# The third dense unit of six stages gets weight tiles of its own, split right behind the norm

## The chip, the cores and the metric

The kernel runs on one core of a Trainium2 chip. Five engines work side by side and meet by semaphores: TensorE (PE in the profile, its weight loads PEld) multiplies, VectorE (DVE), ScalarE (ACT) and GpSimd (POOL) do the elementwise work, SyncE (SP) issues most of the DMAs. The metric is the time of one launch on the device in microseconds. The kernel before takes 1724.36 us, the median of three runs (1722.74 to 1725.32).

## The reference

One step of a two-layer trunk, in float32, on 640 tokens (512 of a latent grid, 128 of a context). Width 1024, FFN width 2816. The two token groups share all weights and differ in their modulation. Cut to what matters:

```python
def trunk_layer(x, mod, g_mix_pre, g_mix_post, g_ffn_pre, g_ffn_post, w_ffn_in, w_ffn_conv, w_ffn_out, mixer):
    shift1, scale1, gate1, shift2, scale2, gate2 = mod      # silu(c) @ w_mod + b_mod
    h = rmsnorm(x, g_mix_pre) * (1 + scale1) + shift1
    y, ctx_state = mixer(h)          # h @ w_in, attention (layer 0: also pooling), @ w_out
    x = x + gate1 * rmsnorm(y, g_mix_post)
    h = rmsnorm(x, g_ffn_pre) * (1 + scale2) + shift2
    x = x + gate2 * rmsnorm(conv_ffn(h, w_ffn_in, w_ffn_conv, w_ffn_out), g_ffn_post)
    return x, ctx_state

def conv_ffn(h, w_in, w_conv, w_out):
    u = h @ w_in                     # then 3 taps along the tokens
    gate, val = jnp.split(u, 2, axis=-1)
    return (jax.nn.silu(gate) * val) @ w_out
```

## The kernel before, in words

**Units.** Activations lie feature-major: 8 chunks of 128 features by 640 tokens. A dense stage is cut into *units*, each 128 output features for all tokens; units are numbered through the program (`UNITS`). A stage is, in each layer, the input projection ("in", 12 or 18 units), the mixer's output ("mix", 8), the first half of the FFN's gate and value columns ("fin0", 22), its down projection ("fout0", 8), and the second halves ("fin1", "fout1").

**Three products for one.** Weights and activations are held as a high part (rounded to the multiplier's format) and a low residual; a product is high x high + high x low + low x high. So a unit over 8 chunks is 8 x 3 x 2 = 48 matmuls, the 2 being the two halves of 320 tokens, which go to two PSUM banks (`bankA[s]`, `bankB[s]`). The high part of a weight is a ScalarE copy (`hi`, L519 to L523, into `whi`), the residual a VectorE subtraction (`lo`, L836 to L840, into `wlo`).

**Two slots.** `raw`, `whi`, `wlo` and the bank pairs have two slots, and unit u uses slot s = u mod 2. For unit u, SyncE loads `raw[s]` once `lo` of unit u-2 is done (`s_lo`); `hi` waits until unit u-2 has been multiplied (`s_unit`), `lo` for `hi` (`s_hi`), TensorE for `lo` and for both halves of unit u-2 to be read out of the banks (`s_fa`, counted by ScalarE's `copy_a`; `s_fb`, counted by VectorE's `copy_b`). In a running stage the split of unit u+2 therefore happens while unit u+1 is multiplied. Each engine works off its own program in order, so the code of an engine is its queue: ScalarE's body of a pair is, for each slot, wait for the unit, `hi` of the unit after next, then the bank copy; VectorE's is bank copy, then `lo`, then what the stage adds.

**The start of a stage.** In the input projections and in "fin0" the activations come chunk by chunk out of `pre_norm`, in "mix" out of the split of the mixer's output (`mix_in_hi`, `mix_in_lo`). The first two units are multiplied together, chunk by chunk as these arrive (`first_pair`, `mix_pair`, `pair_chunk` L1619): for a chunk six matmuls of slot 0, then six of slot 1. Both units thus end within six matmuls of each other, and the third unit, which uses slot 0 again, can be split only then.

**What else hangs on it.** Behind `pre_norm` of layer 0, ScalarE runs a SiLU over a wide copy of the conditioning vector (`wide_silu`, L635 to L637); VectorE waits for it (`s_cwsilu`) before its modulation products (`mod_chunk`, L843 to L850), which fill layer 0's stages; in "mix" of layer 0 four of them (two chunks) follow each unit's split. A change of ScalarE's function set is a table load in its program. The loops over pairs are hardware loops (`Fori`).

Of the kernel before, what the change touches and what calls it, by code (L numbers as in the profile page):

```python
# [26 lines left out]
F32 = mybir.dt.float32  # L27
# [36 lines left out]
ADDED = ((0, "mix"), (0, "fout1"), (1, "mix"), (1, "fout1"))  # L64

# [46 lines left out]
UNITS_OF = attention_units()  # L112

# [5 lines left out]
def program(nc, a, o):  # L119
    with ExitStack() as ctx:  # L120
# [88 lines left out]
        assert pos[0] <= region_f + 2 * FH * NT * 4  # L209
        cwide1 = at("cwide1", [P, 2, 1024], F32, region_c)  # L210
# [307 lines left out]
        def _(act):  # L518
# [5 lines left out]

            def pairs(phase, evac):
# [107 lines left out]
            pre_norm(0, 0, True)  # L633

# [8 lines left out]
            def unit_pair(pair, dsts, k2=KD, scale=1.0):  # L643
                for s in range(2):
                    act.wait_ge(s_unit, 2 * pair + (s + 3))
                    hi(s, k2, pair + 1)
# [78 lines left out]
            def mix_in_hi(layer):  # L725

                act.wait_ge(s_oe, (30, 70)[layer])
                for c in range(KD):
                    nc.scalar.activation(hh[:, c, :], y[:, c, :], ACT.Copy).then_inc(s_oth, 1)
                load_sqrt()  # L730
# [59 lines left out]
            pre_norm(0, 2)  # L790
            wide_silu(cwide1, 2)
# [3 lines left out]
            pre_norm(1, 0)  # L795


            p1 = UNITS[(1, "in")][0] // 2
            with act.Fori(0, 4) as h:
# [28 lines left out]
            pre_norm(1, 2)  # L828
            ffn(1)
# [4 lines left out]
        def _(dve):  # L834
            V = nc.vector

            def lo(s, kk, u):

                dve.wait_ge(s_hi, u + 1)
                V.tensor_tensor(wlo[:, s, 0:kk * P], raw[:, s, 0:kk * P], whi[:, s, 0:kk * P].bitcast(F32),  # L840
                                ALU.subtract).then_inc(s_lo, 1)
# [22 lines left out]
            def run(phase, evac, after=None):  # L864
# [6 lines left out]
                def body(h, k2, extra):  # L871
                    for s in range(2):
                        u = 2 * h + (u0 + s)
                        dve.wait_ge(s_unit, u + 3)
                        evac(h, s, u, lambda: lo(s, k2, u + 2) if k2 is not None else None)
                        if extra is not None:
                            extra(h, s)
                if knext == kk and after is None:
                    with dve.Fori(0, n // 2) as h:
                        body(h, kk, None)  # L880
                else:
                    with dve.Fori(0, n // 2 - 1) as h:
# [3 lines left out]
            def run_all(phase, evac, after):  # L886
# [4 lines left out]
                for k in range(n):  # L891
# [4 lines left out]
                    evac(h, s, u0 + k, lambda: lo(s, k2, u0 + k + 2) if k2 is not None else None)  # L896
# [14 lines left out]
            def unit_pair(pair, dsts, k2=KD, after=None, scale=None):  # L911
                for s in range(2):
                    dve.wait_ge(s_unit, 2 * pair + (s + 3))
                    copy_b(dsts[s], s, scale)
                    lo(s, k2, 2 * pair + (s + 2))
# [108 lines left out]
            pre_norm(0, 0, True)  # L1024

# [12 lines left out]
            def first_early():  # L1038
                for s in range(2):
                    dve.wait_ge(s_unit, s + 3)  # L1040
                    copy_b((apad[s][:, PAD + HT:PAD + NS], apad[s][:, AP0:AP0 + NP]), s)
                    lo(s, KD, s + 2)
# [136 lines left out]
            def mix_in_lo(layer):  # L1179
# [5 lines left out]
                for c in range(KD):  # L1185
                    low(c)

# [111 lines left out]
            pre_norm(0, 2)  # L1299
            ffn(0)  # L1300
            post_norm(0, 3)
            pre_norm(1, 0)
            p1 = UNITS[(1, "in")][0] // 2
# [41 lines left out]
            pre_norm(1, 2)  # L1345
            ffn(1)
# [154 lines left out]

# [456 lines left out]
```

## Time and profile before

| | |
|---|---|
| median of three runs | 1724.36 us |
| span of the profiled execution | 1720.7 us |
| what lies around the span, against the median | 3.7 us |
| TensorE busy | 1601.5 us, 93% of the span |
| VectorE busy | 1097.6 us, 64% |
| ScalarE busy | 716.9 us, 42% |
| GpSimd busy | 132.3 us, 8% |
| HBM traffic | 93 GB/s over the span |

The profile is one execution; its times are microseconds from the first instruction. The profiled execution has no time of its own beside its span, so the table sets it against the median. A matmul's row shows its whole way through the array, 0.31 us for 320 columns, while the next one starts about 0.15 us after it; so a busy TensorE in this table is a TensorE that always has a matmul under way. In brackets behind an instruction stands the idle time of its engine just before it and who ended it.

### The profile page before, as it was taken

How to read it: one execution, taken by the hardware profiler on the slowest of the kernel's cores; microseconds unless marked ns; L12 is line 12 of the kernel's file. 1: busy time of each engine (PE TensorE's matmuls, PEld its weight loads, DVE VectorE, ACT ScalarE, POOL GpSimd, SP SyncE). 2: the span in 40 equal slices, each digit the busy share in tenths (PEclk: the TensorE clock that was granted, in tenths of full speed). 3: DMA queues.
4: the chain of work that ended last, by engine and by line, in shares of the span. 5: the costliest groups of instructions: out<-in, count | busy, mean ns of one | idle time of the engine just before them, and what ended most of it. 6: DMA issues, size and time to landing. Idle time of an engine off the chain costs nothing.

```text
span 1720.7 us, 31763 instructions
## 1 busy us (share of the span) xinstructions
PE 1601.5 (93%) x11837; PEld 1535.5 (89%) x11837; DVE 1097.6 (64%) x2060; ACT 716.9 (42%) x1189; POOL 132.3 (8%) x133
## 2 busy tenths in 40 slices
PE   7798998879999999999889979989799999999996
PEld 4797887869999999999879967779699999999996
DVE  5796766957777767778853248853666642466534
ACT  6532664264443134442251147652565531344410
POOL 1431110010000000000100032500100000000001
PEclk9898999999999999999999989999999999999998
DMA  9233002503334533345422120102022221222211
GB/s 362 83 127 106 2 2 92 193 10 117 115 112 165 177 120 110 110 144 188 147 80 73 62 65 2 45 7 80 13 75 81 79 85 61 71 73 74 91 67 61
DMA packets 43773, 160.33 MB, mean 93 GB/s; under 512 B 5184, under 2 KB 6208, under 8 KB 43440
## 3 DMA queue, kind: packets, MB, share of 16 engines
q1 hardware_dynamic: 40896, 152.00, 26.5%
q0 software_dynamic: 1584, 6.38, 1.1%
q8 instruction: 49, 0.80, 0.2%
q10 hardware_dynamic: 1216, 0.92, 0.2%
q14 instruction: 28, 0.23, 0.0%
HBM read 155.74 MB, written 3.54 MB: 93 GB/s over the span
## 4 chain that ended last, share of the span: by engine, by line
PE 76%; DVE 10%; issue 4%; ACT 2%; DMA 2%; POOL 0%; ACTq 0%; DVEq 0%; POOLq 0%; SPq 0%
PE ps L1498 28%; PE ps L1499 28%; PE ps L1676 4%; PE ps L1705 3%; PE ps L1533 3%; PE ps L1691 3%; DMA work<-in_wmodt 2%; DVE work L848 2%; PE ps L1625 1%; PE ps L1626 1%; DVE wlo L840 1%; DVE work L927 1%; DVE ring L848 1%; DVE x L961 1%; PE ps L1512 1%
## 5 line engine op out<-in xcount | busy, mean ns | idle before, releaser
L523 ACT ACTIVATE whi<-raw 128x1024 fp32r<-128x1024 f32 (+1 forms) x166 | 185.7, 1121 | 578.7 <-PE ps L1499 495.9
L1498 PE MATMUL ps<-hh,whi 128*128 128x320 f32 x928 | 288.7, 311 | 15.3 <-DVE wlo L840 15.3
L1499 PE MATMUL ps<-hh,whi 128*128 128x320 f32 x928 | 287.9, 310 | 0.0
L1498 PE MATMUL ps<-hl,whi 128*128 128x320 f32 x928 | 287.7, 310 | 0.0
L1499 PE MATMUL ps<-hl,whi 128*128 128x320 f32 x928 | 287.7, 310 | 0.0
L1499 PE MATMUL ps<-hh,wlo 128*128 128x320 f32 x928 | 287.7, 310 | 0.0
L1498 PE MATMUL ps<-hh,wlo 128*128 128x320 f32 x928 | 287.7, 310 | 0.0
L840 DVE TENSOR_TENSOR wlo<-raw,whi 128x1024 fp32r<-128x1024 f32 (+1 forms) x166 | 218.4, 1318 | 74.8 <-ACT whi L523 74.5
L1498 PEld LDWEIGHTS ps<-hh,whi 128*128 128x128 f32 x928 | 175.1, 189 | 17.1 <-DVE wlo L840 17.1
L1498 PEld LDWEIGHTS ps<-hl,whi 128*128 128x128 f32 x928 | 175.3, 189 | 0.0
L1499 PEld LDWEIGHTS ps<-hh,whi 128*128 128x128 f32 x928 | 175.2, 189 | 0.0
L1498 PEld LDWEIGHTS ps<-hh,wlo 128*128 128x128 f32 x928 | 175.1, 189 | 0.0
L1499 PEld LDWEIGHTS ps<-hh,wlo 128*128 128x128 f32 x928 | 175.0, 189 | 0.0
L1499 PEld LDWEIGHTS ps<-hl,whi 128*128 128x128 f32 x928 | 175.0, 189 | 0.0
L689 ACT ACTIVATE pb<-pb,stat 128x640 f32<-128x640 f32 (+3 forms) x140 | 92.1, 660 | 9.6 <-DVE stat L1120 9.5
L768 ACT ACTIVATE work<-work,wconv 128x642 f32<-128x642 f32 x88 | 73.5, 835 | 52.9 <-DVE work L905 34.7
L1498 PE MATMUL ps<-ffh,whi 128*128 128x320 f32 x308 | 95.2, 309 | 0.0
L1499 PE MATMUL ps<-ffh,whi 128*128 128x320 f32 x308 | 95.2, 309 | 0.0
L1498 PE MATMUL ps<-ffl,whi 128*128 128x320 f32 x308 | 95.2, 309 | 0.0
L1499 PE MATMUL ps<-ffl,whi 128*128 128x320 f32 x308 | 95.2, 309 | 0.0
L1498 PE MATMUL ps<-ffh,wlo 128*128 128x320 f32 x308 | 95.2, 309 | 0.0
L1499 PE MATMUL ps<-ffh,wlo 128*128 128x320 f32 x308 | 95.2, 309 | 0.0
(219 smaller groups left out, 3169.6 us busy)
## 6 DMA issues: line engine op xcount, KB each, us to landing
raw<-in_w SPq DMA_DIRECT2D x134, 512.0 KB, 3.5
work<-in_wmodt SPq DMA_DIRECT2D x54, 512.0 KB, 3.6
raw<-in_w SPq DMA_DIRECT2D x32, 704.0 KB, 4.2
ring<-in_wmodt SPq DMA_DIRECT2D x26, 512.0 KB, 3.7
work<-in_wmod SPq DMA_DIRECT2D x16, 512.0 KB, 6.0
work<-in_rpb POOLq DMA_DIRECT2D x8, 448.0 KB, 4.2
x<-in_x SPq DMA_DIRECT2D x8, 320.0 KB, 6.6
out_x<-x SPq DMA_DIRECT2D x8, 320.0 KB, 2.2
```

What stands on the lines that cost most here:

```text
L523: nc.scalar.activation(whi[:, s, 0:kk * P], raw[:, s, 0:kk * P], ACT.Copy).then_inc(s_hi, 1)
L689: nc.scalar.activation(probs, probs, ACT.Exp, bias=negm, scale=-1.0, accum_out=sums[:, job.unit, half:half + 1]).then_inc(s_p, 1)
L768: nc.scalar.activation(cb[s], ub[s][:, 1:1 + CW], ACT.Copy, scale=wconv[:, bass.ds(2 * h + (2 * f0 + s), 1), 1]).then_inc(s_c1, 1)
L840: V.tensor_tensor(wlo[:, s, 0:kk * P], raw[:, s, 0:kk * P], whi[:, s, 0:kk * P].bitcast(F32), ALU.subtract).then_inc(s_lo, 1)
L848: last = V.scalar_tensor_tensor(out=out, in0=ring[b], scalar=1.0, in1=cwide[:, st, :], op0=ALU.mult, op1=ALU.mult, accum_out=mod[:, st, ba ...
L927: V.tensor_tensor(tn[s], chunk(src, k), inverse_rows, ALU.mult).then_inc(s_t, 1)
L1498: T.matmul(bankA[s], slot(w, s, k), h[:, k, 0:HT], start=st, stop=sp_)
L1499: last = T.matmul(bankB[s], slot(w, s, k), h[:, k, HT:NT], start=st, stop=sp_)
L1533: last = T.matmul(out, h[:, k, t * P:(t + 1) * P], w[:, :, k * P:(k + 1) * P], start=k == 0 and n == 0, stop=k == KD - 1 and n == 2)
L1676: ins = T.matmul(scores_of(job, c, c + w), q[job.rows, job.pair, job.q0:job.q0 + P], k[job.rows, job.kslot, k0:k0 + w], start=n == 0, stop ...
L1691: T.transpose(turned_probs[half][:, c:c + P], pb[j % 4][:, c:c + P], ident[:, :])
L1705: T.matmul(values_bank[job.rows, 0:P], v[:, t, job.v_col:job.v_col + DH], pts[:, job.half, c:c + P], start=i == 0, stop=i == len(keys) - 1)
```

## The change

Two new tiles, `third_hi` and `third_lo`, are laid over a stretch of the FFN region that no one uses at the starts of these stages. In six stages ("in", "mix" and "fin0" of both layers; `THIRD` lists the units) the third unit is split into them: ScalarE runs `hi_third` right behind the norm's last high part or behind the mixer output's, VectorE runs `lo_third` right behind the last residual. The waits on the slot's previous unit (`s_unit`) fall away for it. TensorE multiplies that unit from the new tiles (`third`), still in banks of slot 0, and still behind `s_fa` and `s_fb`. The usual `hi` and `lo` are left out for these six units, and the first round of the loops concerned is written out in front of them on ScalarE, VectorE and TensorE. Amounts of work are the same.

```diff
+THIRD = [UNITS[p][0] + 2 for p in ((0, "in"), (0, "mix"), (0, "fin0"), (1, "in"), (1, "mix"), (1, "fin0"))]
...
+        third_hi = at("third_hi", [P, KD * P], F32R, region_f + 4 * 3840)
+        third_lo = at("third_lo", [P, KD * P], F32R, region_f + 4 * 3840 + 4 * KD * P)
...
+            def hi_third(u):
+
+                act.wait_ge(s_raw[0], 16 * (u // 2) + 16)
+                nc.scalar.activation(third_hi[:, :], raw[:, 0, 0:KD * P], ACT.Copy).then_inc(s_hi, 1)
+
...
-                        if k2 is not None:
+                        if k2 is not None and not (isinstance(h, int) and 2 * h + u0 + s + 2 in THIRD):
                             hi(s, k2, h + (u0 // 2 + 1))
                         evac(h, s, 2 * h + (u0 + s))
...
                 h0 = 0
-                if first is not None:
+                if u0_of(phase) + 2 in THIRD or first is not None:
                     h0 = 1
-                    pairs(phase, first)[0](0, kk)
+                    pairs(phase, evac if first is None else first)[0](0, kk)
...
             pre_norm(0, 0, True)
+            hi_third(2)
...
             pre_norm(0, 2)
+            hi_third(u0_of((0, "fin0")) + 2)
             wide_silu(cwide1, 2)
             ffn(0)
...
+            def lo_third(u):
+
+                dve.wait_ge(s_hi, u + 1)
+                V.tensor_tensor(third_lo[:, :], raw[:, 0, 0:KD * P], third_hi[:, :].bitcast(F32),
                                 ALU.subtract).then_inc(s_lo, 1)
...
+                h0 = 0
+                if u0 + 2 in THIRD:
+                    h0 = 1
+                    body(0, kk, after)
...
                 for c in range(KD):
                     low(c)
+                lo_third(u0_of((layer, "mix")) + 2)
...
+            def third(u):
+
+                pe.wait_ge(s_lo, u + 1)
+                pe.wait_ge(s_fa, u + 1)
+                pe.wait_ge(s_fb, u + 1)
+                for k in range(KD):
+                    cols = slice(k * P, (k + 1) * P)
+                    for n, (w, h) in enumerate(((third_hi, hh), (third_hi, hl), (third_lo, hh))):
+                        st, sp_ = k == 0 and n == 0, k == KD - 1 and n == 2
+                        T.matmul(bankA[0], w[:, cols], h[:, k, 0:HT], start=st, stop=sp_)
+                        last = T.matmul(bankB[0], w[:, cols], h[:, k, HT:NT], start=st, stop=sp_)
+                last.then_inc(s_unit, 1)
...
+            def dense_pairs_after(u0, n):
+
+                third(u0)
+                dense(1, u0 + 1)
+                dense_pairs(u0 + 2, n - 1)
+
             first_pair(0, 0)
-            dense_pairs(2, 4)
+            dense_pairs_after(2, 4)
```

ScalarE's program behind the norm of layer 0's input projection, before: the wide SiLU between two table loads, the dummy square root that loads the second table, then the third unit's high part (`whi`) and the first bank copy (`work<-ps`).

```order
L637 ACT_TABLE_LOAD
L637 ACTIVATE cwide_93<-cwide_93 128x2048
L572 ACT_TABLE_LOAD
L572 ACTIVATE std<-ident 128x1
L523 ACTIVATE whi<-raw 128x1024
L555 ACTIVATE work<-ps 128x320
L523 ACTIVATE whi<-raw 128x1024
```

The same place now:

```order
L535 ACTIVATE third_hi<-raw 128x1024
L650 ACT_TABLE_LOAD
L650 ACTIVATE cwide_93<-cwide_93 128x2048
L584 ACT_TABLE_LOAD
L584 ACTIVATE std<-ident 128x1
L567 ACTIVATE work<-ps 128x320
L530 ACTIVATE whi<-raw 128x1024
```

The third unit's high part has moved from behind the SiLU and the table loads to ahead of them; the bank copy stays behind them.

VectorE's program at the start of layer 0's mixer output, before: the output's eight residuals (`hl`), two chunks of modulation products (`ring`), the bank copy, the third unit's residual, the next products.

```order
L1183 TENSOR_TENSOR hl<-y,hh 128x640 x8
L848 SCALAR_TENSOR_TENSOR work,mod<-ring_0_94,cwide_93 128x1024
L848 SCALAR_TENSOR_TENSOR ring_0_94,mod<-ring_0_94,cwide_93 128x1024
L848 SCALAR_TENSOR_TENSOR work,mod<-ring_1_95,cwide_93 128x1024
L848 SCALAR_TENSOR_TENSOR ring_1_95,mod<-ring_1_95,cwide_93 128x1024
L905 COPY y<-ps 128x320
L840 TENSOR_TENSOR wlo<-raw,whi 128x1024
L848 SCALAR_TENSOR_TENSOR work,mod<-ring_2_96,cwide_93 128x1024
```

The same place now:

```order
L1217 TENSOR_TENSOR hl<-y,hh 128x640 x8
L865 TENSOR_TENSOR third_lo<-raw,third_hi 128x1024
L873 SCALAR_TENSOR_TENSOR work,mod<-ring_0_94,cwide_93 128x1024
L873 SCALAR_TENSOR_TENSOR ring_0_94,mod<-ring_0_94,cwide_93 128x1024
L873 SCALAR_TENSOR_TENSOR work,mod<-ring_1_95,cwide_93 128x1024
L873 SCALAR_TENSOR_TENSOR ring_1_95,mod<-ring_1_95,cwide_93 128x1024
L936 COPY y<-ps 128x320
L873 SCALAR_TENSOR_TENSOR work,mod<-ring_2_96,cwide_93 128x1024
```

The residual has moved ahead of the first products; between the bank copy and the next products nothing is left.

ScalarE's program at the start of layer 1's first FFN half, before: the loop's entry, a table load, the third unit's high part, the bank copy, the middle tap of the convolution.

```order
L550 UNCONDITIONAL_BRANCH
L550 ISA
L521 ISA
L522 ISA
L523 ACT_TABLE_LOAD
L523 ACTIVATE whi<-raw 128x1024
L761 REGISTER_ALU
L555 ACTIVATE work<-ps 128x320
```

The same place now:

```order
L535 ACTIVATE third_hi<-raw 128x1024
L567 ACTIVATE work<-ps 128x320
L783 ACTIVATE work<-work,wconv 128x642
L530 ACTIVATE whi<-raw 128x1024
L567 ACTIVATE work<-ps 128x320
L783 ACTIVATE work<-work,wconv 128x642
L787 ACT_TABLE_LOAD
L787 ACTIVATE work<-work 128x642
```

The first round stands ahead of the loop, and the table load ahead of the high part is gone, here and in the loop's later rounds; the one ahead of the gate's SiLU remains, once.

## Rows read from the trace of the kernel before

**Rows 1.** Chain of waits: share of the span by engine.
```profile
PE 76%; DVE 10%; issue 4%; ACT 2%; DMA 2%; POOL 0%; ACTq 0%; DVEq 0%; POOLq 0%; SPq 0%
```

**Rows 2.** Waits of TensorE, one line: us in total, times, longest us.
```profile
PE ps L1498 <- DVE wlo L840: 15.3, 7, 3.7
```

**Rows 3.** Timeline of TensorE: start us, us, instruction, in brackets idle before and releaser.
```profile
70.37 0.42 PE L1498 MATMUL ps<-hh,whi 128*128 128x320 f32 x1 [3.73 <-DVE wlo L840]
...
101.39 0.41 PE L1498 MATMUL ps<-hh,whi 128*128 128x320 f32 x1 [1.05 <-DVE wlo L840]
...
293.98 0.42 PE L1498 MATMUL ps<-hh,whi 128*128 128x320 f32 x1 [1.61 <-DVE wlo L840]
...
387.79 0.41 PE L1498 MATMUL ps<-hh,whi 128*128 128x320 f32 x1 [2.55 <-DVE wlo L840]
...
887.62 0.42 PE L1498 MATMUL ps<-hh,whi 128*128 128x320 f32 x1 [1.72 <-DVE wlo L840]
...
1159.23 0.42 PE L1498 MATMUL ps<-hh,whi 128*128 128x320 f32 x1 [1.61 <-DVE wlo L840]
...
1247.89 0.42 PE L1498 MATMUL ps<-hh,whi 128*128 128x320 f32 x1 [2.98 <-DVE wlo L840]
```

**Rows 4.** Timeline of TensorE: first matmul of the unit after the third.
```profile
1166.38 0.31 PE L1498 MATMUL ps<-hh,whi 128*128 128x320 f32 x1
...
1256.57 0.31 PE L1498 MATMUL ps<-hh,whi 128*128 128x320 f32 x1
```

**Rows 5.** Windows: length, busy of PE, PEld, DVE, ACT, POOL; granted clock; DMA.
```profile
71.60:74.90 3.30, 3.30 (x14) 3.30 (x14) 3.30 (x5) 0.00 (x0) 3.22 (x2) 0.51 0.49 149
389.00:392.40 3.40, 3.40 (x15) 3.40 (x15) 3.25 (x5) 1.64 (x3) 0.00 (x0) 0.52 0.76 296
...
1249.20:1252.50 3.30, 3.30 (x15) 3.30 (x14) 3.21 (x5) 1.79 (x3) 0.00 (x0) 0.51 0.42 149
...
540.00:640.00 100.00, 100.00 (x684) 100.00 (x683) 70.40 (x109) 23.89 (x31) 0.00 (x0) 1.00 0.46 159
```

**Rows 6.** Timeline of ScalarE, layer 0's input projection, behind the norm.
```profile
63.38 1.28 ACT L637 ACT_TABLE_LOAD   x1
64.68 1.91 ACT L637 ACTIVATE cwide<-cwide 128x2048 f32<-128x2048 f32 x1
...
68.01 1.04 ACT L523 ACTIVATE whi<-raw 128x1024 fp32r<-128x1024 f32 x1
68.96 0.42 ACT L555 ACTIVATE work<-ps 128x320 f32<-128x320 f32 x1
```

**Rows 7.** Timeline of VectorE and TensorE, layer 0's mixer output, start and end.
```profile
291.53 0.49 DVE L905 COPY y<-ps 128x320 f32<-128x320 f32 x1 [4.99 <-PE ps L1626]
...
293.84 1.22 DVE L848 SCALAR_TENSOR_TENSOR work<-ring,cwide 128x1024 f32<-128x1024 f32 x1
...
341.03 0.58 PE L1558 MATMUL ps<-onesd,work 128*128 128x128 f32 x1 [4.54 <-DVE work L1218]
```

**Rows 8.** Timeline of ScalarE and VectorE, layer 0's first FFN half.
```profile
383.61 1.92 ACT L637 ACTIVATE cwide<-cwide 128x2048 f32<-128x2048 f32 x1
...
385.93 0.56 DVE L905 COPY work<-ps 128x192 f32<-128x192 f32 x2 [2.60 <-ACT cwide L637]
```

**Rows 9.** Timeline of ScalarE and VectorE, layer 1's input projection.
```profile
882.22 0.74 ACT L595 ACTIVATE hh<-work 128x640 f32 x1
...
885.14 0.56 DVE L907 TENSOR_SCALAR qk<-ps 128x192 f32<-128x192 f32 x2 [1.31 <-PE ps L1626]
```

**Rows 10.** Timeline of ScalarE and VectorE, layer 1's first FFN half.
```profile
1241.22 0.74 ACT L595 ACTIVATE hh<-work 128x640 f32 x1
...
1244.23 1.28 ACT L523 ACT_TABLE_LOAD   x1 [2.27 <-PE ps L1626]
...
1244.16 0.56 DVE L905 COPY work<-ps 128x192 f32<-128x192 f32 x2 [1.17 <-PE ps L1626]
1246.61 1.23 DVE L840 TENSOR_TENSOR wlo<-raw,whi 128x1024 fp32r<-128x1024 f32 x1 [1.90 <-ACT whi L523]
```

More of the change, by code:

```diff
@@ L112, with u0_of @@
 UNITS_OF = attention_units()
+def u0_of(phase):
+    return UNITS[phase][0]
 def kchunks(phase):
@@ L645, in unit_pair @@
                     act.wait_ge(s_unit, 2 * pair + (s + 3))
-                    hi(s, k2, pair + 1)
+                    if not (isinstance(pair, int) and 2 * pair + s + 2 in THIRD):
+                        hi(s, k2, pair + 1)
                     copy_a(dsts[s], s, scale)
@@ L729, in mix_in_hi @@
                     nc.scalar.activation(hh[:, c, :], y[:, c, :], ACT.Copy).then_inc(s_oth, 1)
+                hi_third(u0_of((layer, "mix")) + 2)
                 load_sqrt()
@@ L795, in _ @@
             pre_norm(1, 0)
+            hi_third(u0_of((1, "in")) + 2)
             p1 = UNITS[(1, "in")][0] // 2
-            with act.Fori(0, 4) as h:
+            unit_pair(p1, [part(qk, s, 0, HT) for s in range(2)], scale=-SCALE)
+            with act.Fori(1, 4) as h:
                 unit_pair(h + p1, [part(qk, 2 * h + s, 0, HT) for s in range(2)], scale=-SCALE)
@@ L828, in _ @@
             pre_norm(1, 2)
+            hi_third(u0_of((1, "fin0")) + 2)
             ffn(1)
@@ L874, in body @@
                         dve.wait_ge(s_unit, u + 3)
-                        evac(h, s, u, lambda: lo(s, k2, u + 2) if k2 is not None else None)
+                        done = k2 is None or (isinstance(u, int) and u + 2 in THIRD)
+                        evac(h, s, u, lambda: None if done else lo(s, k2, u + 2))
                         if extra is not None:
                             extra(h, s)
+                h0 = 0
+                if u0 + 2 in THIRD:
+                    h0 = 1
+                    body(0, kk, after)
                 if knext == kk and after is None:
-                    with dve.Fori(0, n // 2) as h:
+                    with dve.Fori(h0, n // 2) as h:
                         body(h, kk, None)
                 else:
-                    with dve.Fori(0, n // 2 - 1) as h:
+                    with dve.Fori(h0, n // 2 - 1) as h:
                         body(h, kk, after)
@@ L895, in run_all @@
                     dve.wait_ge(s_unit, u0 + k + 3)
-                    evac(h, s, u0 + k, lambda: lo(s, k2, u0 + k + 2) if k2 is not None else None)
+                    done = k2 is None or u0 + k + 2 in THIRD
+                    evac(h, s, u0 + k, lambda: None if done else lo(s, k2, u0 + k + 2))
                     after(h, s)
@@ L914, in unit_pair @@
                     copy_b(dsts[s], s, scale)
-                    lo(s, k2, 2 * pair + (s + 2))
+                    if not (isinstance(pair, int) and 2 * pair + s + 2 in THIRD):
+                        lo(s, k2, 2 * pair + (s + 2))
                     if after is not None:
@@ L1299, in _ @@
             pre_norm(0, 2)
+            lo_third(u0_of((0, "fin0")) + 2)
             ffn(0)
@@ L1758, in y_units @@
                     one(0, 1)
+                h0 = 1
+                if phase[1] == "mix":
+                    third(u0 + 2)
+                    one(1, 1)
+                    h0 = 2
                 if phase in ADDED:
-                    with pe.Fori(1, 4) as h:
+                    with pe.Fori(h0, 4) as h:
                         for s in range(2):
```

11 lines of the change are left out of this document (8 added, 3 removed).

## The prediction, made blind

> **What bounds the kernel now.** I read the chain of waits first, then TensorE's waits by releaser, then the timelines around them. TensorE's own lines hold 76% of the chain [rows 1], so the kernel ends earlier only where TensorE's stream gets denser or where the few stretches led by another engine get shorter. Among its waits one line names what the change touches: the units' matmul line waited 15.3 us in all, 7 times, for VectorE's weight residual wlo [rows 2]. Six of the seven are the third unit of six stages; the seventh, 1.05 us at 101.39, is a later unit of the first stage [rows 3]. At each of the six the first pair, whose matmuls alternate between both weight slots, has just ended, and the third unit's high part may only then overwrite slot 0: one ScalarE copy, one VectorE subtraction, with TensorE idle.
>
> These waits cost more than their idle time in three stages. A unit of 48 matmuls takes 1166.38 - 1159.23 = 7.15 us behind the 1.61 us wait, but 1256.57 - 1247.89 = 8.68 us behind the 2.98 us one [rows 3, 4]. The windows show why: behind the waits of 3.73, 2.55 and 2.98 us the granted clock was 0.51 to 0.52 for 3.3 to 3.4 us, the 1.2 GHz level, and 1.00 (2.4 GHz) in steady work [rows 5]. So each such fall costs 8.68 - 7.15 = 1.53 us. Behind the wait of 1.61 us there was none.
>
> **What the change costs and removes.** It moves one high copy (1.04 us [rows 6]) and one residual (1.23 us [rows 10]) per stage to just behind the norm or the mixer output's split, where both engines otherwise wait for the pair. Nothing is computed twice. The third unit then needs two things: its weights, and the banks of the pair's first unit emptied. The second was hidden behind the split and is late next. Its price: a ScalarE copy of 0.42 us [rows 6] and, beside it, VectorE copies of 0.49 or 0.56 us [rows 7, 9]. A matmul's row lasts 0.31 us while the next starts 0.15 us after it (7.15/48), so a wait that goes entirely gives its idle time plus 0.16 us.
>
> *Layer 1's mixer output.* The banks are copied while the pair's last six matmuls run (0.49 us [rows 7] against 6 x 0.15 = 0.9 us). The split falls into idle time: in layer 0's mixer stage VectorE sat 4.99 us idle before its first bank copy even with products ahead of it [rows 7], and here there are none. The whole wait goes: 1.61 + 0.16 = 1.77; I take 1.70, since a latency of under 0.1 us may stay.
>
> *Layer 0's mixer output.* Here TensorE is not the end: at the stage's end it waits 4.54 us for VectorE [rows 7], which runs modulation products between the units. What counts is VectorE's stream. Its first bank copy starts at 291.53 and takes 0.49, the products start at 293.84 [rows 7]; without the residual between them they start at 291.97. Gain 1.87. The residual now stands ahead of the products that open the stage and puts them back by about 1.4 us, inside the 4.99 us of idle; the weights of the next products, which their end requests, were not waited for at 293.84 [rows 7]. Were one of them late by 1.87 us, this term would fall to 0; if TensorE's 4.54 us idle were shorter than the gain, the rest would be lost, which it isn't.
>
> *Layer 1's input projection.* The norm's last high part ends at 882.22 + 0.74 = 882.96, the third's copy at 884.00, its residual at 885.29. The bank copy, at 885.14 before, then starts at 885.30 and ends at 885.86 [rows 9]. TensorE can start at 885.87 instead of 887.62: 1.75.
>
> *Layer 1's first FFN half.* Last high part until 1241.96, third's copy until 1243.00, residual until 1244.25; then the six tiny clears, then the bank copy (1244.16 before, now about 1244.55) until 1245.11 [rows 10]. Start about 1245.15 instead of 1247.89: 2.74. ScalarE's table load of 1.28 us, which stood ahead of the old copy at 1244.23 [rows 10], is no longer in this path: the loop whose table state it mended now begins with the right one. With an idle of some 0.3 us left the clock should hold: 1.53 more. Together 4.27.
>
> *Layer 0's first FFN half.* Here ScalarE runs a SiLU over the wide vector between the norm and the units. The third's copy stands ahead of it and pushes it by 0.95 (from a copy's start to the next instruction's, 68.96 - 68.01 [rows 6]). VectorE's bank copy waits for that SiLU: it started 0.4 us after its end (383.61 + 1.92 = 385.53, 385.93) [rows 8]. Now the SiLU ends at 386.48, the copy starts at 386.55 to 386.90 and ends at 387.11 to 387.46; TensorE starts at 387.15 to 387.5 instead of 387.79. Gain 0.3 to 0.64; I take 0.64, because the 0.4 us look like the loop's start, which now comes later. So most of this wait stays, as a wait for the bank and not for the weight. Its idle is then about 1.9 us, between waits with and without a clock fall; I keep the fall, 0 gained.
>
> *Layer 0's input projection.* The same trap: table load, SiLU, table load, then the unit's copies [rows 6]. The third's copy moves from behind them to ahead of them, so the bank copy at 68.96 hardly moves; it ends at 69.38, and the third unit starts at about 69.44 instead of 70.37: 0.93. The idle stays near 2.8 us, the clock falls as before. Later in this stage VectorE, slowed while GpSimd runs the pooling, makes TensorE wait 1.05 us at 101.39 [rows 3]. VectorE loses a residual from its stream and begins its products at 67.65, when the SiLU ends, instead of just before 70.37: up to 2.6 us ahead, some of it stopped by the copies that wait for TensorE. So between 0.9 (if VectorE still sets the pace) and 0.93 + 1.05 + 1.53 = 3.5 (if both it and the clock fall go). I take 1.7.
>
> Sum: 1.70 + 1.87 + 1.75 + 4.27 + 0.64 + 1.70 = 11.9 us. The profiled span is 1720.7; 3.7 us lie around it up to the median of 1724.36. So 1708.8 of span, 1712.4 on the clock.
>
> *What it adds on the engines' programs.* 12 units of 48 matmuls are written out in front of the loops, and six loops on TensorE now begin inside a running stream rather than behind a wait. In 540 to 640, which holds the entry of the second half's loop and the down projection's, TensorE was busy 100.00 of 100 us [rows 5], so a loop's start costs nothing there: 0, and with the nearest bad case the rival below. The page "Runtime: NRT & Kernel Launch" of the Trainium skill (Instruction fetch mechanics) says that a taken branch out of the fetched window stalls the engine until its page arrives. By that rule six entries could stall; by the row none does, and the sum goes by the row.
>
> The second doubt is the clock. The Trainium skill's "TensorE: Matmul & The Clock Gate" (What's actually happening) says that the monitor runs free of the program, so that the same idle need not always be answered alike. By it the falls left in the first and third stage are a matter of phase. The rows agree so far as the wait of 1.61 us had no fall and those from 2.55 us had one; what lies between no row shows.
>
> **The rivals.**
> *The clock returns everywhere.* If the 1.9 and 2.8 us left in the two SiLU stages bring no fall: 2 x 1.53 more, less what VectorE in the first stage keeps (about half): 2.3. 1710.1. For it: one of the two is below every wait with a fall. Against: 2.8 is above.
> *Only the plain waits go.* VectorE still sets the pace at 101.39, the FFN half keeps its 0.4 us behind the SiLU, and the clock falls in layer 1's FFN half anyway, because the pair itself waits for the norm's chunks: 0.93 + 1.87 + 0.3 + 1.75 + 1.70 + 2.74 = 9.3. 1715.1. For it: the pair is led by the norm there.
> *The wait only moves on by one unit.* The fourth unit's split could be late, since its copies now start at the pair's end. It then has a unit of 7.15 us for 1.04 + 1.23 us plus copies; in layer 0's mixer stage four products of 1.22 us [rows 7] and a bank copy of 0.49 stand ahead of its residual, which leaves 7.15 - 4.9 - 0.5 - 1.2 = 0.5 us. If it were late everywhere by what is won, 1724.4: no change.
> *Slower: the loop entries stall.* Each of the six loops now entered in mid-stream stalls TensorE while its code is fetched. The place is the unit behind the fourth; the price, for which no row has a stall of this kind, is set at the shortest wait it would stand for, 1.61 us [rows 3], with a clock fall of 1.53 behind it: 6 x 3.14 = 18.8 lost against 11.9, 1731.3. It decides from 2 us a loop on. Against it stands the 100 us window.
>
> **How the numbers follow.** The forecast 0.62, clock everywhere 0.15, only the plain waits 0.15, the wait moves on 0.05, slower 0.03. The likeliest gives 1712.4. Other falls of the clock, at the norms, start wherever the shifted program meets them, 1.5 us each way, so the range is 1708.3 to 1717.2. A measurement of this kernel tells about 0.2% (3.4 us) from no change; faster than 1720.9 are the first three and part of what is between: 0.93; same 0.05; slower 0.02.
>
> **What would show it.** In the profile after: no wait of the third unit for a residual in any stage; in layer 0's first and third dense stages a wait of 2 to 3 us that ends with ScalarE's or VectorE's bank copy; no table load at the start of layer 1's FFN half and full clock behind it; in layer 0's mixer stage the products starting about 0.4 us behind the pair. I am wrong if the SiLU stages gain their whole waits, if a new wait stands before the fourth unit, or if TensorE idles at a loop's first matmul.

## The result, and the profile after it

The changed kernel takes 1712.24 us (median of 4 runs, 1707.59 to 1715.19), the one before 1723.55 us (4 runs, 1722.10 to 1725.32): a ratio of 0.9933 [0.9920, 0.9945]. A second set of six runs, told below, gives 0.9935 [0.9923, 0.9947]. The prediction was 1712.4.

The profiled execution of the changed kernel is the slowest of its four (1715.19, span 1713.4; 1.8 us lie around the span). Profile against profile, only 7.3 us are gone (1720.7 to 1713.4). So I compare the two traces stage by stage, from the start of a stage's first pair, and not by clock time.

Waits of TensorE after the change, by what it waits for (us in total, times, longest us):

```profile
PE ps L1549 <- ACT work L567: 2.3, 1, 2.3
PE ps L1549 <- DVE work L936: 2.3, 2, 2.1
PE ps L1536 <- DVE wlo L859: 0.5, 1, 0.5
```

L1549 is the matmul line of the third units, now a line of its own; L567 and L936 are the bank copies of ScalarE and VectorE. The 15.3 us for the residual [rows 2] have become 0.5 us, at the seventh unit of the first stage, and no third unit waits for its weight. What is left of their waits, 4.6 us, is for the bank. The chain of waits, where TensorE held 76% [rows 1], now reads (a q behind an engine's name is its sequencer, "issue" time in which the engine waited for nothing that the profile shows):

```profile
PE 81%; DVE 7%; issue 3%; ACT 2%; ACTq 0%; DVEq 0%; POOL 0%; POOLq 0%
```

Timeline of TensorE after (start us, us, instruction, in brackets idle before and releaser): the first matmul of each of the six third units, and in second place the seventh unit of the first stage, to be laid beside [rows 3].

```profile
72.41 0.61 PE L1549 MATMUL ps<-hh,third_hi 128*128 128x320 f32 x1 [2.33 <-ACT work L567]
...
102.68 0.41 PE L1536 MATMUL ps<-hh,whi 128*128 128x320 f32 x1 [0.47 <-DVE wlo L859]
...
294.90 0.34 PE L1549 MATMUL ps<-hh,third_hi 128*128 128x320 f32 x1
...
388.11 0.38 PE L1549 MATMUL ps<-hh,third_hi 128*128 128x320 f32 x1 [2.11 <-DVE work L936]
...
886.08 0.38 PE L1549 MATMUL ps<-hh,third_hi 128*128 128x320 f32 x1
...
1156.41 0.34 PE L1549 MATMUL ps<-hh,third_hi 128*128 128x320 f32 x1
...
1242.15 0.38 PE L1549 MATMUL ps<-hh,third_hi 128*128 128x320 f32 x1 [0.16 <-DVE work L936]
```

Four of the six have no wait or 0.16 us; the two stages with a SiLU keep 2.33 and 2.11 us. Set against the start of the stage's first pair (TensorE's timeline of either trace; us):

| stage | pair starts, before / after | third unit behind it, before / after | gained there | predicted |
|---|---|---|---|---|
| layer 0 input projection | 50.65 / 53.57 | 19.72 / 18.84 | 0.88 | 0.93 |
| layer 0 mixer output | 276.76 / 279.21 | 17.22 / 15.69 | 1.53 | (VectorE leads) |
| layer 0 first FFN half | 368.69 / 369.44 | 19.10 / 18.67 | 0.43 | 0.64 |
| layer 1 input projection | 867.46 / 867.68 | 20.16 / 18.40 | 1.76 | 1.75 |
| layer 1 mixer output | 1140.60 / 1140.91 | 18.63 / 15.50 | 3.13, of it 1.4 clock | 1.70 |
| layer 1 first FFN half | 1228.94 / 1226.04 | 18.95 / 16.11 | 2.84 | 2.74 |

The clock has moved as well. Windows after (length; busy time of PE, PEld, DVE, ACT, POOL; granted clock; DMA share and GB/s), the first, second and fourth at the places of [rows 5]:

```profile
72.50:75.80 3.30, 3.30 (x14) 3.30 (x14) 3.30 (x6) 1.08 (x2) 1.78 (x2) 0.54 0.19 79
389.90:393.20 3.30, 3.30 (x15) 3.30 (x14) 3.26 (x6) 1.71 (x3) 0.00 (x0) 0.54 0.02 6
994.10:997.40 3.30, 3.30 (x19) 3.30 (x18) 0.00 (x0) 0.00 (x0) 0.00 (x0) 0.54 0.63 245
1242.20:1252.20 10.00, 10.00 (x69) 10.00 (x70) 8.16 (x13) 7.43 (x10) 0.00 (x0) 1.00 0.35 107
```

It still falls behind the two waits that stayed, and holds in layer 1's first FFN half. But this trace has a fall at 994 that the trace of before has not: there the same place ran at full clock.

```profile
994.60:998.00 3.40, 3.40 (x28) 3.40 (x29) 0.00 (x0) 0.00 (x0) 0.00 (x0) 1.00 0.86 290
```

Layer 1's mixer output shows the opposite. Its pair begins behind a wait of 2.43 us for the split of the mixer's output, in both traces; in the trace of before it ran at half clock for 6.7 us (first window), in the trace after for 3.3 us (second and third):

```profile
1140.00:1146.70 6.70, 6.10 (x23) 6.13 (x24) 5.60 (x8) 5.47 (x9) 0.00 (x0) 0.51 0.01 2
```
```profile
1140.70:1144.00 3.30, 3.09 (x12) 3.12 (x13) 3.30 (x6) 3.30 (x6) 0.00 (x0) 0.52 0.02 5
1144.20:1147.50 3.30, 3.30 (x25) 3.30 (x24) 2.85 (x4) 2.53 (x4) 0.00 (x0) 1.00 0.00 0
```

From its first matmul to its last the pair is 1.36 us shorter (16.71 and 15.35), which is why the table takes 1.4 us out of that stage's 3.13. Ahead of the first pair, where nothing is changed, it went the other way: TensorE's dense work from 21 us on began at half clock after the change, and the pair starts 2.92 us later. The same window in the trace of before and after:

```profile
24.00:27.00 3.00, 3.00 (x22) 2.02 (x21) 1.50 (x2) 2.29 (x3) 0.00 (x0) 1.00 1.04 406
```
```profile
24.00:27.00 3.00, 3.00 (x13) 2.61 (x14) 0.96 (x1) 0.14 (x1) 0.00 (x0) 0.50 1.04 406
```

So a pair of single profiles says little of 11 us in all, and each stage has to be read by itself.

### The profile page after: what moved, and what is told of

It is laid out like the page before. It is cut to its first block, busy times and chain, and to the rows that moved or that the text cites. A ratio compares the mean times of both kernels' runs of the same rounds, so it can differ in the third digit from the quotient of the medians.

```text
span 1713.4 us, 31655 instructions
## 1 busy us (share of the span) xinstructions
PE 1603.4 (94%) x11837; PEld 1537.1 (90%) x11837; DVE 1095.0 (64%) x2060; ACT 691.7 (40%) x1170; POOL 129.9 (8%) x133
## 4 chain that ended last, share of the span: by engine, by line
PE 81%; DVE 7%; issue 3%; ACT 2%; ACTq 0%; DVEq 0%; POOL 0%; POOLq 0%
PE ps L1536 29%; PE ps L1537 29%; PE ps L1733 4%; PE ps L1762 3%; PE ps L1584 3%; PE ps L1748 3%; PE ps L1600 1%; PE ps L1563 1%; PE ps L1562 1%; DVE work L959 1%; DVE ring L873 1%; PE ps L1676 1%; DVE wlo L859 1%; PE ps L1677 1%; PE ps L1549 1%
## 5 line engine op out<-in xcount | busy, mean ns | idle before, releaser
L530 ACT ACTIVATE whi<-raw 128x1024 fp32r<-128x1024 f32 (+1 forms) x160 | 179.4, 1124 | 572.6 <-PE ps L1537 489.3
L1536 PE MATMUL ps<-hh,whi 128*128 128x320 f32 x880 | 272.0, 309 | 0.5 <-DVE wlo L859 0.5
L1537 PE MATMUL ps<-hl,whi 128*128 128x320 f32 x880 | 271.9, 309 | 0.0
L1537 PE MATMUL ps<-hh,wlo 128*128 128x320 f32 x880 | 271.9, 309 | 0.0
L1536 PE MATMUL ps<-hl,whi 128*128 128x320 f32 x880 | 271.9, 309 | 0.0
L1536 PE MATMUL ps<-hh,wlo 128*128 128x320 f32 x880 | 271.9, 309 | 0.0
L1537 PE MATMUL ps<-hh,whi 128*128 128x320 f32 x880 | 271.9, 309 | 0.0
L859 DVE TENSOR_TENSOR wlo<-raw,whi 128x1024 fp32r<-128x1024 f32 (+1 forms) x160 | 211.2, 1322 | 58.1 <-ACT whi L530 57.9
L1536 PEld LDWEIGHTS ps<-hh,whi 128*128 128x128 f32 x880 | 165.2, 188 | 0.7 <-DVE wlo L859 0.7
L1537 PEld LDWEIGHTS ps<-hh,whi 128*128 128x128 f32 x880 | 165.2, 188 | 0.0
L1537 PEld LDWEIGHTS ps<-hl,whi 128*128 128x128 f32 x880 | 165.2, 188 | 0.0
L1537 PEld LDWEIGHTS ps<-hh,wlo 128*128 128x128 f32 x880 | 165.2, 188 | 0.0
L1536 PEld LDWEIGHTS ps<-hl,whi 128*128 128x128 f32 x880 | 165.2, 188 | 0.0
L1536 PEld LDWEIGHTS ps<-hh,wlo 128*128 128x128 f32 x880 | 165.2, 188 | 0.0
L936 DVE COPY work<-ps 128x192 f32<-128x192 f32 (+1 forms) x180 | 49.8, 319 | 77.4 <-PE ps L1537 74.4
```

Source lines behind the costliest of these rows:

```text
L530: nc.scalar.activation(whi[:, s, 0:kk * P], raw[:, s, 0:kk * P], ACT.Copy).then_inc(s_hi, 1)
L936: last = V.tensor_copy(dst, bankB[s][:, f:f + n])
L1536: T.matmul(bankA[s], slot(w, s, k), h[:, k, 0:HT], start=st, stop=sp_)
L1537: last = T.matmul(bankB[s], slot(w, s, k), h[:, k, HT:NT], start=st, stop=sp_)
```

## The experiments

Theory: the six waits for the weight are what is won, less what the bank copies behind the two SiLUs keep. Rivals: the written-out rounds and the table load they save win it; or the fall of the clock behind the waits does. Ratios are against the kernel before, run beside on the same chip, with 95% intervals.

**pe_written_out.** The kernel before, with the first rounds of all six stages written out, on TensorE's program alone:

```diff
+            def dense_pairs_after(u0, n):
+                dense(0, u0)
+                dense(1, u0 + 1)
+                dense_pairs(u0 + 2, n - 1)
...
             first_pair(0, 0)
-            dense_pairs(2, 4)
+            dense_pairs_after(2, 4)
```

> The kernel before with only TensorE's program changed: the third and fourth unit of the six stages written out ahead of the loops, split and tiles as before. Theory (loop entries cost nothing): the six waits stand where they were and as long as they were (3.73, 1.61, 2.55, 1.72, 1.61, 2.98 us), no new wait before the fifth unit, 1723.5 +- 1.5. Rival (a loop entered in mid-stream stalls for its code): a new idle of 1 us or more before each loop's first matmul, 6 x 1.6 to 3.1 us, 1733 or more.

1724.07 us, 1.0005 [0.9995, 1.0015]. Writing the rounds out neither gains nor costs, within 0.15%. The entries of the loops in mid-stream don't stall TensorE: in all six stages the fifth unit, the first of the loop, starts without a wait, 7.04 us behind the fourth. What came unasked is in its timeline and windows: two of the three waits behind which the clock fell in the trace of before are there at their old length, and the clock holds. (In the first stage the wait is 3.11 us, and the clock falls.)

```profile
389.37 0.41 PE L1498 MATMUL ps<-hh,whi 128*128 128x320 f32 x1 [2.54 <-DVE wlo L840]
...
1249.01 0.41 PE L1498 MATMUL ps<-hh,whi 128*128 128x320 f32 x1 [2.98 <-DVE wlo L840]
```
```profile
389.40:396.40 7.00, 7.00 (x48) 7.00 (x49) 6.04 (x9) 2.86 (x6) 0.00 (x0) 1.00 0.69 226
1249.10:1256.10 7.00, 7.00 (x48) 7.00 (x49) 6.04 (x9) 4.24 (x7) 0.00 (x0) 1.00 0.54 151
```

**all_written_out.** The changed kernel with everything written out as it is, but every third unit in the old slot (OWN lists the stages that use the new home):

```diff
+OWN = [UNITS[p][0] + 2 for p in ()]
...
             def third(u):
+                if u not in OWN:
+                    return dense(0, u)
```

> The changed kernel with its written-out first rounds on all three engines, but no tiles of its own: the third unit is split in its slot as before. Theory: five waits as before; in layer 1's first FFN half the table load of 1.28 us ahead of the split is gone with the loop's entry, so this wait is 2.98 - 1.28 = 1.7 us and the clock holds behind it: 1.28 + 1.53 = 2.8 us faster, 1720.7. Rival (that stage's gain comes from the tiles alone): wait 2.98 us, clock falls, 1723.5.

1720.42 us, 0.9983 [0.9974, 0.9992]: 2.6 us by medians (1722.98 for the kernel before), from one stage above all. In layer 1's first FFN half ScalarE's high copy follows on the pair with no table load between, and the third unit waits 1.67 us instead of 2.98 [rows 3]. Timelines of ScalarE and of TensorE:

```profile
1246.10 1.06 ACT L531 ACTIVATE whi<-raw 128x1024 fp32r<-128x1024 f32 x1 [2.25 <-PE ps L1684]
```
```profile
1248.47 0.42 PE L1541 MATMUL ps<-hh,whi 128*128 128x320 f32 x1 [1.67 <-DVE wlo L862]
```

The table load of [rows 10] stood ahead of the old loop's first copy. 2.98 - 1.67 = 1.31 us is its 1.28 us: of the 2.74 us predicted for this stage nearly half comes from writing the round out, not from the new home. The clock holds behind the shorter wait (the unit takes 7.14 us); in pe_written_out it held behind 2.98 us too, so how much of the other 1.3 us is a fall that went isn't shown.

**before_filled_waits.** The kernel before, with matmuls into a stretch of PSUM that nobody reads in the three long waits, so that TensorE is busy through most of each wait while the wait for the weight stays:

```diff
+            def filler(n):
+                for _ in range(n):
+                    T.matmul(psf[:, 3712:4032], hh[:, 0, 0:P], hh[:, 0, 0:HT], start=True, stop=True)
...
             first_pair(0, 0)
+            filler(20)
...
                         first_pair(u0, 8 * (2 * layer + 1))
+                        filler((12, 14)[layer])
```

> The kernel before with 20, 12 and 14 extra matmuls of 320 columns (result thrown away, a free stretch of PSUM) behind the first pair of layer 0's input projection and of both first FFN halves, where the waits of 3.73, 2.55 and 2.98 us stand. The wait for the weight is the same. Theory (the idle makes the clock fall, 1.53 us each): no fall behind these three, the unit takes 7.1 instead of 8.7 us; the two FFN halves give 3.1 us, the input projection less since VectorE sets its pace later: 1720 +- 1.5. Rival (the fall has another cause, or comes back elsewhere by phase): 8.7 us as before, 1723.5.

1722.86 us, 0.9997 [0.9987, 1.0007]: a miss. In its trace the clock holds behind both FFN waits, with the filler in front of them:

```profile
387.63 1.92 PE L1642 MATMUL ps<-hh 128*128 128x320 f32 x12
...
390.35 0.41 PE L1498 MATMUL ps<-hh,whi 128*128 128x320 f32 x1 [0.79 <-DVE wlo L840]
```
```profile
390.40:397.40 7.00, 7.00 (x48) 7.00 (x49) 6.04 (x9) 2.87 (x6) 0.00 (x0) 1.00 0.71 225
1250.20:1257.20 7.00, 7.00 (x48) 7.00 (x49) 6.04 (x9) 4.23 (x7) 0.00 (x0) 1.00 0.51 150
```

Yet nothing is gained that shows. The two FFN waits have no sure fall to begin with (pe_written_out). In the first stage the clock holds too (the third unit takes 7.14 us instead of 8.69), but TensorE's wait for VectorE at the seventh unit grew from 1.05 [rows 3] to 2.37 us, so all of it is given back: the seventh unit starts 50.72 us behind the pair, 50.74 before. The interval leaves room for a gain of 2.2 us, not for the 11: the rival that the clock wins the time has fallen as the main cause, and a share of 1 or 2 us is not excluded.

**four_stages_own and two_silu_stages_own.** As all_written_out, with the new home in the four stages without a SiLU, and in the two with one:

```diff
-OWN = [UNITS[p][0] + 2 for p in ()]
+OWN = [UNITS[p][0] + 2 for p in ((0, "mix"), (1, "in"), (1, "mix"), (1, "fin0"), )]
```
```diff
-OWN = [UNITS[p][0] + 2 for p in ()]
+OWN = [UNITS[p][0] + 2 for p in ((0, "in"), (0, "fin0"), )]
```

> The changed kernel with tiles of its own only in the four stages without a SiLU ahead (both mixer outputs, layer 1's input projection and first FFN half); the two others split in the slot, rounds written out everywhere. Theory (sum of the terms): 1.67 + 1.70 + 1.80 + 2.74 + 0 to 1.53 for the clock = 7.9 to 9.4 faster than the kernel before: 1714.5 +- 1.5. Rival (the two SiLU stages carry a share like the others, a sixth each of 11.3): 1715.5 or more.

> The changed kernel with tiles of its own only in the two stages with a SiLU ahead, layer 0's input projection and first FFN half; rounds written out everywhere. Theory: 0.9 (to 1.7 with VectorE's lead) + 0.4 for the two, and 1.3 for the table load that the written-out round drops in layer 1: 2.6 to 3.4 faster than before: 1719.7 +- 1.5. Rival (their waits of 3.73 and 2.55 us go whole): 1715.

1715.28 us, 0.9958 [0.9946, 0.9970], and 1718.35 us, 0.9976 [0.9966, 0.9987]. By medians that is 7.4 and 4.4 us (1722.72 for the kernel before on this chip); both hold the written-out table load, 1.3 us, so together 7.4 + 4.4 - 1.3 = 10.5, beside 10.4 for the changed kernel on the same chip (after_again below, 1722.72 - 1712.30). With the 2.6 us that all_written_out measured in place of the 1.3 they are 9.2. The stages add up within what these intervals can tell, some 2 us each. Both times lie in the theory's ranges; the first is also only 0.2 us from its rival's, so it doesn't tell the two apart, while the second lies 3.4 us from its rival. In the second kernel the first stage's third unit waits 2.85 us with no fall behind it, and the seventh unit starts at 98.23, 47.78 us behind the pair:

```profile
69.28 0.39 PE L1556 MATMUL ps<-hh,third_hi 128*128 128x320 f32 x1 [2.85 <-ACT work L570]
...
98.23 0.41 PE L1541 MATMUL ps<-hh,whi 128*128 128x320 f32 x1 [0.56 <-DVE wlo L862]
```
```profile
69.40:76.40 7.00, 7.00 (x49) 7.00 (x50) 5.38 (x9) 1.06 (x2) 4.57 (x3) 1.00 0.49 132
```

**after_again.** The changed kernel once more, for a second trace and a closer ratio.

> The changed kernel once more, on the same chip as the next three, since its first four runs spread over 7.6 us. Theory (the spread is falls of the clock at other places): 1712.2 +- 1.5; the unit starts behind each first pair as in the first profile to 0.3 us wherever the clock did not fall (third unit 18.8, 15.6, 18.7, 18.4, 15.6, 16.1 us behind the pair's start). Rival (the first median was luck of few runs): 1714 or more.

1712.30 us, 0.9935 [0.9923, 0.9947]. The third units lie where they did (18.84, 15.68, 18.66, 18.43 and 16.10 us behind their pairs, layer 1's mixer output at 16.82 with more of its pair at half clock), but the clock does not fall behind the wait that was kept in layer 0's first FFN half:

```profile
385.75 0.38 PE L1549 MATMUL ps<-hh,third_hi 128*128 128x320 f32 x1 [2.12 <-DVE work L936]
```
```profile
385.80:392.80 7.00, 7.00 (x48) 7.00 (x49) 5.95 (x9) 3.61 (x6) 0.00 (x0) 1.00 0.41 146
```

2.11 us with a fall and 2.12 us without, in two executions of one program.

**silu_later_fin0.** If the SiLU keeps the wait in layer 0's first FFN half, moving it behind the pair's copies must free it. VectorE's wait for the SiLU, which stood ahead of its own bank copy, moves to the first product that needs it:

```diff
                     if s == 1:
+                        if isinstance(h, int) and h + f0 == 0:
+                            wide_silu(cwide1, 2)
...
             hi_third(u0_of((0, "fin0")) + 2)
-            wide_silu(cwide1, 2)
             ffn(0)
```

> The changed kernel with the wide SiLU of layer 0's first FFN half moved behind the bank copies of the first pair (ScalarE), and VectorE's wait for it moved to its first user, the first modulation product of the stage. Theory (the wait of 2.11 us left there is ScalarE's SiLU before the bank copy, and the clock falls behind it): the wait goes to 0.2 us or less and the fall with it: 2.1 + 0.2 + 1.5 = 3.7 us faster than the changed kernel, 1708.5 +- 2. Rival (only the idle goes, a later wait takes it): 1710 to 1712.

1709.99 us, 0.9926 [0.9913, 0.9939]. The third unit starts 16.69 us behind the pair instead of 18.67, without a wait, and ScalarE's bank copy now runs ahead of the SiLU. Timelines of TensorE and ScalarE:

```profile
382.63 0.39 PE L1553 MATMUL ps<-hh,third_hi 128*128 128x320 f32 x1
```
```profile
381.93 0.44 ACT L567 ACTIVATE work<-ps 128x320 f32<-128x320 f32 x1 [1.43 <-DVE work L1318]
...
387.94 1.91 ACT L650 ACTIVATE cwide<-cwide 128x2048 f32<-128x2048 f32 x1
```

So the SiLU kept 1.98 us of TensorE's start. The fifth and sixth unit give 0.36 us of it back (they start 7.30 and 7.14 us behind the units before them, 7.04 in the changed kernel). As a time it is within the noise: 0.9926 beside 0.9933 and 0.9935 for the changed kernel.

**silu_and_table_later.** silu_later_fin0, and in the first stage the table load behind the SiLU goes behind the pair's copies too:

```diff
             wide_silu(cwide0, 1)
-            load_sqrt()
...
             unit_pair(0, [apad[s][:, PAD:PAD + HT] for s in range(2)])
+            load_sqrt()
```

> The changed kernel with the SiLU of layer 0's first FFN half moved as in the run before, and in layer 0's input projection the dummy square root with its table load moved behind the first pair's bank copies. The bank copy then follows the SiLU directly, about 1.4 us sooner. Theory (VectorE sets the pace later in that stage): the third unit starts 1.4 us sooner, the seventh unit waits longer for its residual, and 0 to 1 us of it arrives: 1709.5 +- 1.5. Rival (TensorE's start decides): 1.4 us and the clock's fall arrive, 1707.

1707.09 us, 0.9908 [0.9895, 0.9921]: the fastest, and it beats both kernels (the changed one took 1712.30 beside it). My theory, that VectorE would keep most of this table load's time, fell; its rival had the number. The trace beside that of silu_later_fin0, from which it differs by the table load alone, shows why; in neither does the clock fall behind this wait. VectorE's products and its copy for the third unit, here:

```profile
67.74 1.23 DVE L874 SCALAR_TENSOR_TENSOR work<-ring,cwide 128x1024 f32<-128x1024 f32 x1 [0.87 <-ACT cwide L650]
...
75.51 0.68 DVE L939 TENSOR_SCALAR qk<-ps,small 128x192 f32<-128x192 f32 x2 [0.40 <-PE ps L1554]
```

and in silu_later_fin0:

```profile
68.04 1.23 DVE L874 SCALAR_TENSOR_TENSOR work<-ring,cwide 128x1024 f32<-128x1024 f32 x1 [0.91 <-ACT cwide L650]
...
77.32 0.68 DVE L939 TENSOR_SCALAR qk<-ps,small 128x192 f32<-128x192 f32 x2 [1.89 <-PE ps L1554]
```

The products start 16.93 us behind the pair in both (its first matmul is at 50.81 and 51.11). But with the table load in its old place VectorE then waited 1.89 us for TensorE's late third unit; here it waits 0.40. VectorE had slack that my theory had spent. The third unit starts 17.32 instead of 18.83 us behind the pair, the seventh 46.33 instead of 47.78: 1.45 of 1.51 us arrive. The rival's second part, a fall of the clock that goes with the wait, is not in these two traces.

**silu_behind_both.** Further in the same direction: SiLU and table load both behind the pair's copies, so that the third unit has no wait at all.

```diff
-            wide_silu(cwide0, 1)
-            load_sqrt()
...
             unit_pair(0, [apad[s][:, PAD:PAD + HT] for s in range(2)])
+            wide_silu(cwide0, 1)
+            load_sqrt()
```

VectorE's first two products, which need the SiLU, follow behind both bank copies.

> As the fastest version so far (SiLU of the first FFN half moved), but in layer 0's input projection the whole SiLU with both table loads stands behind the first pair's bank copies, and VectorE's first two modulation products behind the fourth unit's residual. Nothing is then ahead of the third unit: it starts at the pair's end, 1.0 us sooner than in the run with only the table load moved, and the clock does not fall. Theory (VectorE's products set the pace of this stage): they start about 4 us later, the seventh unit waits 3 us or more for its residual, 1709.5 +- 1.5. Rival (TensorE's start decides, as the last run suggested): the seventh unit waits 0.6 us as before and 1 us arrives, 1706.

1713.40 us beside 1725.53 for the kernel before on that chip: 0.9931 [0.9917, 0.9946], that is 0.0023, or 4.0 us, worse than silu_and_table_later (the intervals just overlap; the traces part clearly). The theory's 1709.5 +- 1.5 was too low beside this chip's 1725.53 (0.9931 of the 1722.72 above would be 1710.8), but VectorE now leads, as it said: its products start at 73.41, 21.32 us behind the pair instead of 16.93. The third unit gains 0.84 us, and TensorE gives all of it back, with interest, at the fifth unit (1.07 us of wait) and the seventh, which starts 49.89 us behind the pair instead of 46.33.

```profile
73.41 1.53 DVE L874 SCALAR_TENSOR_TENSOR work<-ring,cwide 128x1024 f32<-128x1024 f32 x1 [2.33 <-ACT cwide L650]
```
```profile
101.98 0.63 PE L1540 MATMUL ps<-hh,whi 128*128 128x320 f32 x1 [3.68 <-DVE wlo L860]
```

Of the three orders tried in this stage the best leaves the third unit a wait of 1.04 us and starts it 1.5 us sooner than the changed kernel does, and VectorE follows that almost whole.

## Why the prediction was right, step by step

*The plain waits.* Layer 1's input projection gained 1.76 (predicted 1.75) and layer 1's mixer output 1.77 without the clock (1.70): its third unit starts 0.15 us behind the start of the pair's last matmul, 1.92 before. VectorE's timeline shows how the first came out: the residual runs while the pair still does, and the bank copy follows it at once, where [rows 9] had it idle for 1.31 us.

```profile
884.18 1.23 DVE L865 TENSOR_TENSOR third_lo<-raw,third_hi 128x1024 fp32r<-128x1024 f32 x1
885.37 0.56 DVE L938 TENSOR_SCALAR qk<-ps 128x192 f32<-128x192 f32 x2
```

*Layer 0's mixer output.* As predicted VectorE's stream is what counts: its products follow on the bank copy after 0.40 us instead of 2.31 [rows 7], and TensorE still waits 4.48 us at the end (4.54 before). From the pair's start to that end it is 62.60 us instead of 64.27: 1.67, predicted 1.87. The missing 0.2 lies in the trace of before, whose first pair is shorter than elsewhere (15.30 us, in the other traces of the old slot 15.53 to 15.55). In those four traces the end comes at 64.49 to 64.51: 1.9.

```profile
294.22 0.49 DVE L936 COPY y<-ps 128x320 f32<-128x320 f32 x1 [4.09 <-PE ps L1677]
294.62 1.22 DVE L873 SCALAR_TENSOR_TENSOR work<-ring,cwide 128x1024 f32<-128x1024 f32 x1
...
341.81 0.58 PE L1609 MATMUL ps<-onesd,work 128*128 128x128 f32 x1 [4.48 <-DVE work L1253]
```

*The trap behind the SiLU.* In both stages the wait stayed as a wait for the bank copy, as foretold; silu_later_fin0 and silu_and_table_later show it by moving the SiLU and the table load out of the way. Layer 0's first FFN half gained 0.43, not 0.64: the SiLU was pushed as computed, and VectorE's copy followed its end (385.31 + 1.91 = 387.22) after 0.18 us, so some of the 0.4 us which I put down to the loop's start had stayed.

```profile
387.40 0.56 DVE L936 COPY work<-ps 128x192 f32<-128x192 f32 x2 [2.10 <-issue]
```

In the first stage ScalarE's program is the one expected, with the third's copy at its head, and the gain at the third unit was 0.88 (0.93); at the seventh unit, 50.74 us behind the pair before and 49.11 after, it had become 1.63 (1.70).

```profile
66.20 1.04 ACT L535 ACTIVATE third_hi<-raw 128x1024 fp32r<-128x1024 f32 x1
67.26 1.28 ACT L650 ACT_TABLE_LOAD   x1
68.56 1.92 ACT L650 ACTIVATE cwide<-cwide 128x2048 f32<-128x2048 f32 x1
70.49 1.28 ACT L584 ACT_TABLE_LOAD   x1
71.89 0.42 ACT L567 ACTIVATE work<-ps 128x320 f32<-128x320 f32 x1
```

*Layer 1's first FFN half.* 2.84 us at the third unit (2.74). ScalarE goes from the third's copy to the bank copy with no table load; all_written_out puts 1.3 us of this down to that load alone.

```profile
1238.96 1.04 ACT L535 ACTIVATE third_hi<-raw 128x1024 fp32r<-128x1024 f32 x1
...
1241.44 0.44 ACT L567 ACTIVATE work<-ps 128x320 f32<-128x320 f32 x1 [1.44 <-DVE work L1313]
```

*The step that failed.* "With an idle of some 0.3 us left the clock should hold: 1.53 more." It held in this trace, and set against the trace of before the term is there in full. But it took for granted that before it always fell there. In pe_written_out the same 2.98 us had no fall; over all traces, waits from 2.1 to 3.0 us are followed by one or not. The Trainium skill's "TensorE: Matmul & The Clock Gate" (What's actually happening) has the monitor run free of the program, so that the same idle need not be answered alike; the waits of 2.11 and 2.12 us in two executions of the changed kernel agree. Counted over the traces, with the third unit in the old slot and in the new home (start of a later unit behind the first pair, us):

| stage, unit | old slot | new home | gain of the means | predicted |
|---|---|---|---|---|
| layer 0 input projection, seventh | 50.74, 50.68, 50.71, 50.72 (all with a fall) | with a fall 49.11, 48.91; without 47.78, 47.78 | 2.3 | 1.70 |
| layer 0 first FFN half, fourth | with a fall 27.77, 27.76; without 26.22, 26.23 | with 27.31; without 25.76, 25.78 | 0.7 | 0.64 |
| layer 1 first FFN half, fourth | with a fall 27.63; without 26.42 | 23.21 to 23.40 in six traces, none with a fall | 3.8 | 4.27 |

The old slot is in before, pe_written_out, all_written_out and four_stages_own (last row: the first two alone, which have the table load), the new home in after, after_again, two_silu_stages_own and silu_later_fin0 (second row: the first three; last row: the six that have it there). So layer 1's first FFN half is worth 4.2 to 4.4 us beside an execution with the fall and 3.0 to 3.2 beside one without. The first stage shows the reverse. Before, VectorE kept the seventh unit back to some 50.7 us behind the pair (waits of 1.05, 1.23 and, with the filler, 2.37 us), and a fall behind the third cost nothing there: 50.68 to 50.74 us whether the third unit took 7.14 us (before_filled_waits, 50.72) or 9.88. After the change VectorE is ahead there, and the stage gives 2.9 us without a fall, 1.6 to 1.8 with one; the falls which I left at 0 gave something after all.

With these means the sum is 2.3 + 1.9 + 0.7 + 1.76 + 1.77 + 3.8 = 12.2 us; measured are 11.2 to 11.5, with an interval from 9.1 to 13.3 (0.9935 [0.9923, 0.9947]). Nothing more needs to be explained, as far as two to six traces to a mean can tell. before_filled_waits agrees: of its three falls one cost nothing and two come in about half of the executions, so some 1.5 us were to be won, and its interval reaches to 2.2. That the forecast came within 0.2 us is in part luck: the first stage was 0.6 us too low, this term about half a microsecond too high.

*The loop entries.* 0, as the 100 us window said; pe_written_out measured it, and the rival "slower" has fallen with it. *The fourth unit* never waited for its split.

*Around the span.* The 3.7 us there were too many: 1.8 us lie around it in every run since, so the profiled execution of before was simply one of the faster (1720.7 + 1.8 = 1722.5).

## What to carry to other kernels

When a wait names one releaser, look for the second condition that the waiting instruction has, price it from the same timeline, and ask which instruction on that releaser's engine stands ahead of it: here the bank copies behind a SiLU and a table load kept 4.4 of 15.3 us, and moving two instructions won 5 us more. A gain on one engine is worth as much as the engine it feeds has slack, which is read from the waits of that second engine (1.89 us here, of which 1.49 were used), and one step too far gives back more than it won. Don't book a clock fall seen in one trace as time to be won: count it in several executions first.

## What was not expected of the hardware

- After a wait of a given length TensorE's clock fell from 2.4 to 1.2 GHz in one execution and not in another: at 2.98 us (before: 0.51 for 3.3 us; pe_written_out: 1.00), at 2.55 and 2.54 us (the same two traces), at 2.11 and 2.12 us (after: 0.54; after_again: 1.00). In the first stage it fell behind 2.86 to 3.73 us in all four traces with the split in the slot, and in the new home it held behind 2.85 and 2.60 us (two_silu_stages_own, silu_later_fin0) and fell behind 2.33 and 2.27 (after, after_again). Filling three such waits gained nothing that shows, 0.9997 [0.9987, 1.0007].
- Writing out a loop's first round removed a table load of 1.28 us ahead of the loop's first copy, worth 1.31 us at TensorE's wait in that stage.
